# Two DRAM tables of gates for even and odd heads, cleared from DRAM beside the mixer branches, 104 scattered tokens instead of 96, and a reordered merge and projection

## The reference

```
gate   = sigmoid(z_gate + gate_b)
merged = gate[0] * (y_rw @ p_rw) + gate[1] * (y_ml @ p_ml)   # two mixer branches, 512 wide each
x      = x + merged @ w_out
tok    = rmsnorm(x) ;  q = tok @ w_q                          # 8 heads
s      = q . sub_keys          ; top 16 of each half, then the top 16 of the 256 sums, per token and head
gate   = softmax(best)                                        # 8 x 16 = 128 experts per token
act    = gelu(u_emb[expert] . tok) * gate                     # 16384 experts = 128 x 128
out    = rmsnorm(x + sum over k of act[k] * v_emb[expert[k]])
```

## Time and profile before

| | |
|---|---|
| runs | 2194.47 us median of 3 (2194.3 to 2196.11) |
| profiled execution | 2196.2 us, of which the profile's span is 2194.4 us |
| PE busy | 2147.0 us, 98% of the span |
| DVE, ACT, POOL busy | 1601.9, 1038.2, 335.1 us |
| stages (us from the start) | mixers about 1070 to 1321, merge and projection to 1417, "early" items to 1562, "mid" items to 1820, output stage to 2187 |

### The profile page before, as it was taken

The page is one execution under the profiler, slowest core; times in us unless marked ns, Lnnn a source line. Parts: engine busy times, 40 slices in busy tenths (PEclk is TensorE's granted clock), DMA queues, the critical chain, the costliest instruction groups (busy, mean ns, idle before and its releaser), DMA issues. The chain is left out here.

```text
span 2194.4 us, 46339 instructions
## 1 busy us (share of the span) xinstructions
PE 2147.0 (98%) x18016; PEld 2034.0 (93%) x18016; DVE 1601.9 (73%) x3068; ACT 1038.2 (47%) x1687; POOL 335.1 (15%) x199
## 2 busy tenths in 40 slices
PE   9999999999999999999899999999999998999998
PEld 9999989999999998999889989999999997888887
DVE  6665868765875687876686687699799555777776
ACT  5444555443544466554453345454444453333333
POOL 0000000000000000000000000199877871000000
PEclk9999999999999999999999999999999999999999
DMA  6553535564556443556332226577555675666664
GB/s 218 181 197 131 195 111 175 181 200 147 168 179 200 136 167 128 175 193 220 117 124 70 79 81 210 170 243 239 154 146 145 178 187 176 204 206 209 206 204 162
DMA packets 134106, 373.70 MB, mean 170 GB/s; under 512 B 44568, under 2 KB 48808, under 8 KB 133808
## 3 DMA queue, kind: packets, MB, share of 16 engines
q1 hardware_dynamic: 118320, 364.95, 50.5%
q0 software_dynamic: 15616, 6.35, 2.4%
HBM read 363.85 MB, written 7.39 MB: 169 GB/s over the span
## 5 line engine op out<-in xcount | busy, mean ns | idle before, releaser
L1180 DVE TENSOR_TENSOR w_lo<-ring,w_hi 128x1024 fp32r<-128x1024 f32 (+1 forms) x301 | 393.3, 1308 | 186.0 <-ACT w_hi L926 185.4
L926 ACT ACTIVATE w_hi<-ring 128x1024 fp32r<-128x1024 f32 (+1 forms) x301 | 337.5, 1126 | 335.2 <-PE ps L554 321.9
L554 PE MATMUL ps<-x_hi,w_hi 128*128 128x272 f32 (+1 forms) x1608 | 460.4, 286 | 1.4 <-DVE x_lo L1251 1.1
L554 PE MATMUL ps<-x_hi,w_lo 128*128 128x272 f32 (+1 forms) x1608 | 458.1, 285 | 0.0
L554 PE MATMUL ps<-x_lo,w_hi 128*128 128x272 f32 (+1 forms) x1608 | 455.8, 283 | 0.0
L554 PEld LDWEIGHTS ps<-x_hi,w_hi 128*128 128x128 f32 x1608 | 302.2, 188 | 4.5 <-DVE w_lo L1180 1.5
L554 PEld LDWEIGHTS ps<-x_lo,w_hi 128*128 128x128 f32 x1608 | 302.0, 188 | 0.2
L554 PEld LDWEIGHTS ps<-x_hi,w_lo 128*128 128x128 f32 x1608 | 302.2, 188 | 0.0
L3391 ACT ACTIVATE v_gated_hi<-ring 128x1024 fp32r<-128x1024 f32 x128 | 135.9, 1062 | 226.8 <-PE ps L3441 226.3
L3176 POOL MEMSET hot_j<- 128x768 f32 x1 | 0.7, 737 | 1417.2 <-POOLq L3000 1417.2
L3441 PE MATMUL ps<-v_gated_hi,gated_gelu_hi 128*128 128x512 f32 x512 | 203.0, 396 | 7.6 <-DVE v_gated_lo L266 7.6
(11 more groups left out here) (531 smaller groups left out, 5279.8 us busy)
## 6 DMA issues: line engine op xcount, KB each, us to landing
ring<-in_gate_up SPq DMA_DIRECT2D x173, 512.0 KB
ring<-in_peer_v SPq DMA_DIRECT2D x128, 512.0 KB
ring<-in_down SPq DMA_DIRECT2D x64, 704.0 KB
ring<-in_peer_u_mid SPq DMA_DIRECT2D x80, 512.0 KB
ring<-in_peer_u_early SPq DMA_DIRECT2D x48, 512.0 KB
ring<-in_w_in SPq DMA_DIRECT2D x46, 512.0 KB
ring<-in_project SPq DMA_DIRECT2D x32, 512.0 KB
ring<-in_da_qk SPq DMA_DIRECT2D x18, 512.0 KB
```

The source lines that it names most:

```text
L554: mm = nc.tensor.matmul(ps[:, bank, 0:ntok], parts[left][:, item % SLOTS, t * P:(t + 1) * P], rhs[right][:, k, 0:ntok], start=start and n ...
L926: A.activation(parts_of(n)[0][:, n % SLOTS, 0:width[n]], ring[:, n % SLOTS, 0:width[n]], ACT.Copy).then_inc(hi_done.sem, 1)
L1180: V.tensor_tensor(parts_of(n)[1][:, n % SLOTS, 0:width[n]], ring[:, n % SLOTS, 0:width[n]], parts_of(n)[0][:, n % SLOTS, 0:width[n]].bitca ...
```

## The change

It does five things. (1) `SCATTERED` goes from 96 to 104, so 152 tokens are left for PE's one-hot groups: 38 groups instead of 40. (2) There are two tables, interleaved in `far_gates`: even heads add into one, odd heads into the other. POOL waits before head hd (from 2 on) for the heads of the same table before it, and not at the end of each head. (3) The table, now 13.6 MB, is cleared by 32 DMAs that copy an input of zeros from DRAM, issued by POOL at the start of the block of the mixers, each after the one before has landed; POOL's memset and the 16 clearing DMAs in the "early" stage are gone. (4) `far_in` holds 2 x 104 floats per row, and DVE first adds the two halves. Before `picked`, DVE writes the index in two operations instead of one. (5) In the projection P3 comes before A0, P5 before A1 and P7 before A2, the first splits are no longer made ahead of the first merge, and DVE's weight split of the next item goes between `merge_sum` and `merge_low`.

```
-SCATTERED = 96
+TABLES = 2
+SCATTERED = 104
-ZERO_PIECES = 16
+ZERO_PIECES = 32
...
-PROJECT = ["P0", "P1", "P2", "A0", "P3", "P4", "A1", "P5", "P6", "A2", "P7", "B4", "A3", "B5", "B6", "B7"] + [f"Q{i}" for i in range(16)]
+PROJECT = ["P0", "P1", "P2", "P3", "A0", "P4", "P5", "A1", "P6", "P7", "A2", "B4", "A3", "B5", "B6", "B7"] + [f"Q{i}" for i in range(16)]
...  act_program
+                if item:
+                    split_hi(item + NB)
                 if kind == "P":
                     act.wait_ge(merged_sum, m + 1)
                     A.activation(merged[0][:, m, :], total[:, m % 2, :], ACT.Copy).then_inc(merged_hi, 1)
-                split_hi(item + NB)
+                if not item:
+                    split_hi(NB)
...  dve_program
-            for n in range(PROJECT_AHEAD, NB):
-                split_lo(n)
+            low = PROJECT_AHEAD
...
                 dve.wait_ge(used, item + 1)
                 if kind == "P":
-                    merge(m)
+                    merge_sum(m)
+                    split_lo(low)
+                    low += 1
+                    merge_low(m)
...
-                if name == "P7":
-                    split_lo(item - 1 + NB)
-                split_lo(item + NB)
+                for n in range(low, item + NB + 1):
+                    split_lo(n)
+                low = max(low, item + NB + 1)
...
+        def clear_far_gates(pool):
+            far_pieces = far_gates.rearrange("(n p c) o -> n p (c o)", n=ZERO_PIECES, p=P)
+            for n in range(ZERO_PIECES):
+                pool.dma_start(far_pieces[n], a["zeros"]).then_inc(far_cleared.sem, 16)
+                pool.wait_ge(far_cleared.sem, 16 * (n + 1))
...  experts_in_pool
-            pool.memset(zeros, 0.0).then_inc(zeros_set.sem, 1)
-            pool.wait_ge(zeros_set.sem, 1)
             for i in range(w.n):
                 take_lo(pool, w, u_parts, i, i % SLOTS)
-                if i % 2 and i // 2 < ZERO_PIECES:
-                    pool.dma_start(far_pieces[i // 2], zeros).then_inc(far_landed.sem, 16)
...
             for hd in range(PH):
+                if hd >= TABLES:
+                    pool.wait_ge(far_landed[hd % TABLES].sem, 16 * TOPK * (hd // TABLES))
                 for n in range(TOPK * hd, TOPK * hd + TOPK):
...
-                pool.wait_ge(far_landed.sem, 16 * (ZERO_PIECES + TOPK * (hd + 1)))
...  experts_out_sp
-                sp.wait_ge(far_landed.sem, 16 * (ZERO_PIECES + SEL))
+                sp.wait_ge(spread.sem, TG)
+                for e in range(TABLES):
+                    sp.wait_ge(far_landed[e].sem, 16 * SEL // TABLES)
...  experts_out_dve
-                    V.tensor_tensor(value[:, 0:SCATTERED], value[:, 0:SCATTERED], far_in[:, slot, :], ALU.mult).then_inc(far_used.sem, 1)
+                    V.tensor_tensor(far_in[:, slot, 0, :], far_in[:, slot, 0, :], far_in[:, slot, 1, :], ALU.add).then_inc(far_summed.sem, 1)
+                    dve.wait_ge(far_summed.sem, j + 1)
+                    V.tensor_tensor(value[:, 0:SCATTERED], value[:, 0:SCATTERED], far_in[:, slot, 0, :], ALU.mult).then_inc(far_used.sem, 1)
```

More of the change, by code:

```diff
@@ L3033, in experts_inputs, with peer @@
     return got, base
-def peer(nc, a, out, env, save, inputs, past_inputs):
+def peer(nc, a, out, env, save, inputs, past_inputs, far_gates, far_cleared):
     sb_in, at_phase, tally, ps, h, ring, W, ident, ones = (env[x] for x in ("sb_in", "at_phase", "tally", "ps", "h", "ring", "W", "ident", "ones"))
@@ L3099, in peer @@
         far_gate = nc.alloc_sbuf_tensor_at("far_gate", [P, SEL], F32, offset=at + 4 * SEL)
[L3100 to L3101 removed]
+        far_in = nc.alloc_sbuf_tensor_at("far_in", [P, SLOTS, TABLES, SCATTERED], F32, offset=far_in_at)
         iota4 = iota[:, :].unsqueeze(1).broadcast_to([P, 4, P])
@@ L3312, in experts_in_dve @@
                             total[:, 0, :].unsqueeze(2).broadcast_to([P, PH, TOPK]), ALU.mult)
-            V.tensor_scalar(far_index[:, :], row_f[:, :], float(INDEX_SCALE * SCATTERED), iota_k[:, TOKEN_COLUMN:TOKEN_COLUMN + 1], ALU.mult,
-                            ALU.add).then_inc(picked.sem, 1)
-            dve.wait_ge(far_landed.sem, 16 * ZERO_PIECES)
+            for e in range(TABLES):
+                of_table = [t.rearrange("p (h e k) -> p h e k", e=TABLES, k=TOPK)[:, :, e, :] for t in (far_index[:, :], row_f[:, :])]
+                last = V.tensor_scalar(of_table[0], of_table[1], float(INDEX_SCALE * TABLES * SCATTERED),
+                                       iota_k[:, TOKEN_COLUMN + e:TOKEN_COLUMN + e + 1], ALU.mult, ALU.add)
+            last.then_inc(picked.sem, 1)
             def one_hots(g):
@@ L3360, in peer @@
                 gated_gelu.append(sb_in(c, f"gated_gelu_{part}", [P, 2, SEQ], F32R))
+            assert nc.sbuf_base <= far_in_at
             def experts_out_sp(sp):
                 sp.dma_start(final_g, a["final_g"].rearrange("p (s c) -> p s c", s=SLOTS)).then_inc(loaded.sem, 16)
-                sp.wait_ge(far_landed.sem, 16 * (ZERO_PIECES + SEL))
+                sp.wait_ge(spread.sem, TG)
+                for e in range(TABLES):
+                    sp.wait_ge(far_landed[e].sem, 16 * SEL // TABLES)
                 for i, slot, turn in grouped(sp, wv.n, SLOTS):
@@ L3367, in experts_out_sp @@
                         sp.wait_ge(far_used.sem, i - SLOTS + 1)
-                    sp.dma_start(far_in[:, slot, :], far_chunks[i]).then_inc(far_full[slot].sem, 16)
+                    sp.dma_start(far_in[:, slot, :, :], far_chunks[i]).then_inc(far_full[slot].sem, 16)
                     if not early(i, SLOTS):
@@ L3615, in second_arrays @@
     out["ranks"] = np.tile(np.array(RANKS, np.float32), (P, 1))
-    out["ranks"][:, TOKEN_COLUMN] = np.arange(P)
+    for e in range(TABLES):
+        out["ranks"][:, TOKEN_COLUMN + e] = SCATTERED * e + np.arange(P)
+    out["zeros"] = np.zeros((P, NKEY * NKEY * TABLES * SCATTERED // (ZERO_PIECES * P)), np.float32)
     out["iota_scaled"] = con(np.broadcast_to(np.arange(P, dtype=np.float32) / INDEX_SCALE, (P, P)))
```

32 lines of the change are left out of this document (18 added, 14 removed).

## The result

The changed kernel takes 2220.55 us (median of 4 runs, 2219.89 to 2221.38) against 2194.99 for the kernel before: ratio 1.0114, 95% interval 1.0101 to 1.0126. It is 25.6 us slower, where 2181.0 was forecast and 2191.5 was the upper end. The profiled execution has a span of 2218.8 us.

The account below looks back on a forecast made before the run. PE, busy 98%, was taken as the bound, its output stage waiting for POOL's scatters. 2196.2 - 2.7 (projection) - 1.3 (early) - 1.8 (groups) - 4.7 (gap) - 2.7 (clock) = 2183.0 us profiled, forecast 2181; range 2177 to 2191.5.

Parts of the forecast that it names:

- the price of the width: POOL's scatters: 104 rows instead of 96 add d = 0.06 us each, 7.7 us in all, bounded by 0 and 0.118.
- Rival (c): POOL's scatters: rows worked in lots of 16, seven for six, d = 0.237 us, time 2206.6 us; chance 0.07.
- Its sharper form: POOL's scatter time goes by the fullest share, 6 to 8 rows: d = 0.47 us, 2236.9 us; chance 0.01.
- the rule on shares: Scatter DMAs: 13 engines with 8 rows for 104, 16 with 6 for 96; counted as 0.08 us once.
- rival (a): Scatters hide wholly, d up to 0.037 us, whole gap gone: 2180.1 us; within the forecast's 0.70.
- gap -4.7, clock -2.7: Ahead of the output stage: PE's wait falls from 7.6 to 2.9 us, and 2.7 us of half-clock matmuls go.
- Waits for landings: POOL between heads: two tables leave only the ordinary 0.30 us, taking 14.8 us out of its chain.
- Projection: Reordered items remove 3.2 us of PE's waits and add 0.5 us for `branch`: gain 2.7 us.
- Early stage: POOL loses a memset and 16 clearing DMAs, so two of PE's four waits for POOL go: gain 1.3 us.
- The clears beside the mixers: 13.6 MB of table clears beside the mixers cost nothing, since weight copies there wait for PE, not DMA.
- The second DVE operation of the output stage: The added 0.29 us per item fits into DVE's idle time, so the output stage's pace stays.
- The groups: Two one-hot groups fewer on PE, 0.91 us each: gain 1.8 us.

Follow-up runs that it names:

- e4: The changed kernel, 104 rows kept, with DVE's weight split of the mid items made as two operations of 512 columns; 2197.64 us.
- e5: The changed kernel with DVE's low part of the late mid items cut to 8 of 1024 columns; 2188.63 us.
- e7: The kernel before with 104 scattered rows instead of 96 in its one table, nothing else changed; 2237.07 us.
- e1: The changed kernel with 96 scattered rows instead of 104, all else as changed; 2189.53 us.
- e6: The changed kernel with 96 rows and the first four loads of both tables issued by POOL behind its last scatter, not by SP; 2184.69 us.
- e10: The kernel before with the reordered merge and projection alone (96 rows, one table); 2192.05 us.
- e11: The changed kernel with 128 rows, DVE's split of mid items in two operations, and both tables' first four loads issued by POOL; 2185.57 us.

## Why the prediction was wrong

**The step that failed is the price of the width.** The prediction took d = 0.06 us per scatter, bounded by 0 and 0.118 us, "if all of it is by the row". It measured 1.609 - 1.416 = 0.19 us, outside those bounds. With 24.3 us for the 128 scatters in place of 7.7, the prediction's own sum gives 19.5 us of PE's wait and 2200.6 us, which is already slower than before. The bound assumed a price that grows smoothly with the rows; the runs give 1.42, 1.47 and 1.55 us for 96, 112 and 128 rows, and 1.59, 1.59 and 1.61 for 88, 100 and 104. That is about 0.055 to 0.08 us for 16 more rows where 16 divides them, and some 0.15 to 0.2 us on top where it does not. Rival (c) came nearest in size (0.237 us, 2206.6 us), but its reason, lots of 16 rows, is refuted by 112 rows, which are seven lots like 104 and take 1.47 us. Its sharper form had the right occasion, 104 not being a multiple of 16, but the wrong size (0.47 us, from POOL's time going by the fullest share). The prediction named the rule on shares that speaks against 104, set it down as 0.08 us on one landing, and gave its effect on POOL's issue a chance of 0.01.

The packets of the scatters' queue show what changes with the divisor. Before they were 14336. After (queue, packets, MB, share of 16 engines, over the whole stretch of scatters; the run with 88 rows has the same number of packets):

```profile
q0 software_dynamic: 18432, 0.09, 13.3%
```

With 100 rows:

```profile
q0 software_dynamic: 22528, 0.12, 12.8%
```

With 112 rows:

```profile
q0 software_dynamic: 16384, 0.07, 12.2%
```

Divided by 128 scatters these are 112, 144, 176 and 128 packets, and 144 with 88 rows: 16 x 7, 16 x 9, 16 x 11, 16 x 8 and 16 x 9. If one in each factor closes the transfer on its engine, they leave 6, 8, 10, 7 and 8, and these are 96/16, 104/13, 100/10, 112/16 and 88/11. The rule of the Trainium skill that the prediction cited (DMA: Bandwidth & Descriptors, Why a DMA increments its semaphore by 16 and not by 1), with the largest divisor up to 16 as the number of shares, gives just these quotients, so the trace agrees with it in the size of a share. In their number it doesn't: 13 engines with 104 rows and 16 closing packets would be 120 packets, and 144, 16 times 9, were counted. Which engine took which, no run shows. What the earlier trace rows said, 14336 = 128 x 112, I had read only as a time per packet. The issue time doesn't follow the quotient alone: 8 rows to a share take 1.55 us for 128 rows and 1.61 for 104, and 10 take 1.59. Why POOL takes longer for an uneven number stays open.

**The step that was missing is DVE's hold on POOL.** The prediction counted 1.72 us per scatter and did not ask why the mean in before was 198.2/128 = 1.55 us with a longest of 2.47. Of the 16.4 us above the shortest, 9.2 stood in the late items (scatters begun from 1705 to 1810), and that is this hold. With 1.61 us the scatters fell in step with the items: 41.5 us, of which 32.8 in the late items. Run e4 brings the sum to 18.3 us and e5 to 8.9, with 0.1 left in the late items; e7 shows it in before's kernel. The 6 to 9 us among the groups of gates, before 1705, stay nearly the same in every run, and what holds those was not tested. The range had no case for this: of the 31.8 us by which PE's wait grew, 24.3 are d's and 25.1 the hold's, less 16.7 of idle time, 4.6 of POOL's earlier start and 3.1 of a shorter last landing, and with 6.3 for PE's earlier arrival and 0.6 for the longer chain behind the landing.

**The gap has a second floor.** The sum let PE's wait fall to 2.9 us, and rival (a) to nothing, once the scatters were done. Run e1 shows 6.8 us with the last scatter issued 12 us before PE is ready (1823.4 - 6.8 = 1816.6): SP issues `far_in` behind 2.5 MB of other loads. So even with 96 rows the forecast 2181 wasn't reached: 2189.5 was had, and 2184.7 with e6's mend. The term "gap -4.7, clock -2.7" was read from the last link of the chain alone. The size of the clock's part was right: PE's 1530 matmuls of the output stage take 357.26 us before and 354.52 in e6, where PE doesn't stop ahead of them and the granted clock stays at 1.00, which is 2.7 us; in after, where it was 0.50 when they began, they take 356.17.

**The smaller terms.** Waits for landings: gone, as forecast; POOL's idle time fell by 16.7 us, 14.8 were counted. Projection: waits fell from 3.2 to 0.4 us, 2.8 against 2.7 forecast, with the one wait for `branch` (0.4 us, forecast 0.5) and none for `merged_lo`; e10 shows the gain by itself. From its first matmul to that of the queries the stage became 3.9 us shorter (48.1 to 44.2), 1.1 more than these waits; what the rest is, is not shown. Early stage: wrong. Four waits of 3.4 us stand there without any clears on POOL, so the clears' issues were not their cause. They fall where DVE makes `apart`, 2048 columns with two inputs, and POOL's splits take long beside it (timeline of after):

```profile
1466.74 6.82 POOL L267 TENSOR_TENSOR u_early_lo<-ring,u_early_hi 128x1024 fp32r<-128x1024 f32 x2 [0.26 <-ACT u_early_hi L261]
...
1471.31 4.40 DVE L3312 TENSOR_TENSOR apart<-peer_idx_f,rank 128x2048 f32<-128x2048 f32 x1
1471.34 0.38 PE L284 MATMUL ps<-tok_hi,u_early_hi 128*128 128x256 f32 x1 [0.70 <-POOL u_early_lo L267]
```

Two splits take 6.8 us there, where most pairs take 4.8. Before it was the same: the pair of 1471.35, beside `apart`, took 6.82 us, and it stands right ahead of the wait of 0.50 us that the prediction put down to the clears. That this is the same hold is argued from these rows, not tested. The clears beside the mixers cost nothing that shows: ACT's `w_in_hi` still waits for PE alone (62.2 us, 23 times, against the earlier trace rows). The second DVE operation of the output stage is hidden, as forecast: 433 matmuls per 100 us. The groups came out as counted: PE is ready for the output stage at 1855.1 - 39.4 = 1815.7 instead of 1822.0, 6.3 us sooner, of which 4.3 us are its earlier start of the peer stage (1413.3 instead of 1417.6) and 1.8 the two groups.

## What to carry to other kernels

Before changing the number of partitions of an indirect DMA on POOL, see whether 16 divides it: here 88, 100 and 104 rows all cost more per DMA than 112. Look at the sum of the issues against the count times the shortest, for the difference may be what another engine takes. A stream of POOL issues beside a periodic DVE operation can lock to its period, so that 0.2 us more in the issue cost 0.8 us at each item; breaking DVE's operation in two took 22.9 us off the time here. When the last link of a chain is shortened, read the next one (here SP's order of loads) before counting the whole gap as won.

## What was not expected of the hardware

Scatters of 112 rows are issued faster (1.47 us) than scatters of 88 (1.59). The last scatter takes 3.1 us to land when no weights are being loaded (after) and 6.2 to 6.6 us behind the weights' loads (before, e11). An issue of 1.61 us is stretched to 2.42 by a DVE operation of 1.23 us that began 0.3 us before it. A held one runs as if it had begun 0.13 us before the DVE operation's end, wherever in it it started; one that began up to 0.04 us after the operation wasn't held at all.
